# A transformer layer with pooling and RWKV-7 branches on one core: output product and second feed-forward product as seven block products instead of eight

## The reference, cut to what matters

```python
h = x * (1 + sc1) + sh1                       # x: 512 tokens x 1024, sc/sh/gt: from c @ w_ada
p = h @ w_in
y_pool = pool_branch(...)                     # ends in m @ w_pool_up, 512 x 1024
y_rwkv = rwkv7_branch(...)                    # ends in o @ w_rwkv_up, 1024 x 1024
g_pool, g_rwkv = split(sigmoid(p_gate))
mixed = (g_pool * y_pool + g_rwkv * y_rwkv) @ w_out         # 1024 x 1024
x = layer_norm(ALPHA * x + (1 + gt1) * mixed, ln1_g, ln1_b)
h = x * (1 + sc2) + sh2
f = square(relu(h @ w_ff1)) @ w_ff2           # 1024 x 4096, 4096 x 1024
x = layer_norm(ALPHA * x + (1 + gt2) * f, ln2_g, ln2_b)
```

## Time and profile before

| | us |
|---|---|
| median of 3 runs | 1107.34 |
| lowest, highest | 1106.0, 1109.77 |
| the profiled execution | 1106.47 |
| its span, first to last instruction | 1104.7 |
| matmul busy in the span | 999.9 |
| VectorE, ScalarE, Pool busy | 517.9, 413.8, 401.8 |
| mean granted TensorE clock | 0.957 |

### The profile page before, as it was taken

The page is one execution under the profiler, slowest core; times in us unless marked ns, Lnnn a source line. Parts: engine busy times, 40 slices in busy tenths (PEclk is TensorE's granted clock), DMA queues, the critical chain, the costliest instruction groups (busy, mean ns, idle before and its releaser), DMA issues.

```text
span 1104.7 us, 25425 instructions
## 1 busy us (share of the span) xinstructions
PE 999.9 (91%) x10997; PEld 798.8 (72%) x10997; DVE 517.9 (47%) x620; ACT 413.8 (37%) x500; POOL 401.8 (36%) x236
## 2 busy tenths in 40 slices
PE   1898998898899889997999999889999999999992
PEld 1676777685677678675688888768888888888881
DVE  6636589377748768743231245746112112112217
ACT  0335354356335532524433224375124224214311
POOL 6333412311311131125253443445434434443422
PEclk9799999999999899998899999879999999999996
DMA  9322333223323324321433543304333333333201
GB/s 370 106 77 63 97 117 102 79 79 94 93 79 98 103 60 118 105 76 39 133 100 101 160 114 107 95 1 132 97 94 97 96 96 91 99 95 93 79 1 76
DMA packets 153641, 108.08 MB, mean 98 GB/s; under 512 B 5395, under 2 KB 145601, under 8 KB 153537
## 3 DMA queue, kind: packets, MB, share of 16 engines
q1 hardware_dynamic: 143729, 83.46, 25.9%
q10 hardware_dynamic: 9808, 23.08, 6.9%
HBM read 100.23 MB, written 2.10 MB: 93 GB/s over the span
## 4 chain that ended last, share of the span: by engine, by line
PE 47%; DVE 4%; DMA 1%; ACT 1%; issue 0%; SPq 0%; POOL 0%; DVEq 0%; ACTq 0%; POOLq 0%
PE set L1757 23%; PE bank L1757 20%; PE bank L1859 1%; PE set L1859 1%; DVE G L1319 1%; DMA w_raw<-in_w_rwkv_up_dram 1%; DVE xt L1388 1%; DVE xt L1390 1%; PE set L1821 0%; DVE t L1304 0%; PE set L1838 0%; PE set L1607 0%; PE set L1606 0%; DVE aa L1322 0%; DVE stat L1348 0%
## 5 line engine op out<-in xcount | busy, mean ns | idle before, releaser
L560 POOL TENSOR_TENSOR w_lo<-w_raw,w_hi 128x1024 fp32r<-128x1024 f32 (+2 forms) x87 | 200.4, 2303 | 439.2 <-ACT w_hi L641 399.2
L616 POOL TENSOR_TENSOR w_lo<-w_raw,w_hi 128x1024 fp32r<-128x1024 f32 x48 | 115.8, 2413 | 145.9 <-ACT w_hi L936 145.7
L1460 PE MATMUL bank<-h_hi,w_hi 128*128 128x512 f32 x256 | 109.3, 427 | 2.1 <-POOL w_lo L560 2.0
L641 ACT ACTIVATE w_hi<-w_raw 128x1024 fp32r<-128x1024 f32 (+2 forms) x75 | 75.5, 1006 | 82.9 <-PE set L1757 43.6
L669 ACT ACTIVATE Q<-set 128x1024 f32<-128x1024 f32 x56 | 57.4, 1026 | 130.7 <-PE set L1514 73.8
L936 ACT ACTIVATE w_hi<-w_raw 128x1024 fp32r<-128x1024 f32 x60 | 63.7, 1061 | 110.7 <-PE bank L1757 53.9
L1460 PE MATMUL bank<-h_hi,w_lo 128*128 128x512 f32 x256 | 103.3, 403 | 0.3 <-issue 0.3
L1460 PE MATMUL bank<-h_lo,w_hi 128*128 128x512 f32 x256 | 103.5, 404 | 0.0
L1355 DVE TENSOR_TENSOR f<-t 128x512 f32<-128x512 f32 x32 | 26.4, 825 | 125.9 <-ACT t L945 125.5
L1757 PE MATMUL bank<-h_hi,w_hi 128*128 128x512 f32 x192 | 76.5, 398 | 0.0
L1757 PE MATMUL set<-y_hi,w_hi 128*128 128x512 f32 x192 | 76.1, 396 | 0.0
(11 more groups left out here) (328 smaller groups left out, 2030.3 us busy)
## 6 DMA issues: line engine op xcount, KB each, us to landing
w_raw<-in_w_ff_dram SPq DMA_DIRECT2D x64, 512.0 KB, 3.9
w_raw<-in_w_in_dram SPq DMA_DIRECT2D x46, 512.0 KB, 3.8
y<-in_w_ada_dram ACTq DMA_DIRECT2D x20, 512.0 KB, 4.0
ada<-in_w_ada_dram SPq DMA_DIRECT2D x16, 512.0 KB, 9.6
Q<-in_w_ada_dram ACTq DMA_DIRECT2D x12, 512.0 KB, 4.3
w_raw<-in_w_rwkv_up_dram SPq DMA_DIRECT2D x8, 512.0 KB, 4.3
w_raw<-in_w_out_dram SPq DMA_DIRECT2D x8, 512.0 KB, 3.8
xtok<-in_x_dram SPq DMA_DIRECT2D x4, 512.0 KB, 9.9
```

Source lines behind the costliest of these rows:

```text
L560: link(pool.tensor_tensor(part_of(k, w_lo), part_of(k, w_raw), part_of(k, w_hi).bitcast(F32), ALU.subtract), "lo_ready")
L616: again(pool.tensor_tensor(part_of(k, w_lo), part_of(k, w_raw), part_of(k, w_hi).bitcast(F32), ALU.subtract), "lo_ready")
L641: link(act.activation(part_of(k, w_hi), part_of(k, w_raw), ACT.Copy), "hi_ready")
L1460: mm = pe.matmul(o, w, hx, start=(m == 0), stop=(m == 3 * KT - 1))
```

## The change

**The seven products.** Left operand (tokens x features) and right operand (weights) are cut into 2 x 2 blocks, and the product is made by the scheme of Strassen and Winograd with seven block products instead of eight. One **unit** takes 512 of the inner features: left 512 tokens x 512, in halves of 256 tokens and 256 features; right 512 x 1024, in four quarters `B11`, `B12`, `B21`, `B22` of 256 x 512. The output product is two units, the second feed-forward product eight. A unit needs four sums of weights (`T1 = B12 - B11`, `T3 = B22 - B12`, `T2 = B22 - T1`, `T4 = B21 - T2`; VectorE, 128 x 1024 each), four sums of the left halves (`a_sum`, 128 x 256 for each of two groups of features), and seven products (`quarters`) of 2 x 2 x 3 = 12 matmuls, so 84 where the eight blocks took 96 for the same part. Now the activations are the stationary side and 512 columns of weights move.

**Layout.** The result is tokens x features. Products that share an output are accumulated in the same bank and read in between: `take` adds a bank to the tile `acc_out`, unscaled, 14 times a unit. The gate (`1 + gt1`, `1 + gt2`) is now a row over features: 16 transposes of a broadcast column in the last slots of the recurrence and two ScalarE copies make `gate1` and `gate2`. In the last unit of each product `last_takes` multiplies by the gate and adds to `res` (`merged`, `taken_last`), and takes the statistics with `bn_stats`, for both layer norms. `x_again` is no longer turned, and nothing is turned back; instead the normalised `x` is turned for `h2` (32 transposes). `ln1_g` and `ln1_b` are folded into the residual by VectorE (`residual`, 8 instructions) and Pool (8).

**Who makes what.** Of the eleven lo parts of a feed-forward unit (four chunks of `w_ff1`, m = 0 to 3, seven forms of `w_ff2`, m = 4 to 10) VectorE makes m = 2 to 6 (`low_tile`, while chunks are computed), Pool the others (mostly while the seven products run). In the output units Pool makes all. VectorE also makes the lo parts of the left side (`low_raw`, `low_sums`).

**Order.** TensorE does the first output unit after `pool_up(5)` and the second after `pool_up(7)`. A unit of the feed-forward stage is four chunks of `w_ff1` (24 matmuls each) and the seven products. The loop has six or seven turns by engine instead of two or three.

```diff
-        mix_hi, mix_lo = sb("mix_hi", [P, KT, S], F32R), sb("mix_lo", [P, KT, S], F32R)
+        a_hi, a_lo = sb("a_hi", [P, 7, 2, S // 2], F32R), sb("a_lo", [P, 7, 2, S // 2], F32R)
+        a_sum = sb("a_sum", [P, 4, S // 2])
...
+        FORMS = ("B11", "B21", "T2", "T1", "T3", "B22", "T4")
+        FORM_RAW = dict(B11=3, B21=5, T2=3, T1=8, T3=4, B22=6, T4=5)
...
+        PRODUCTS = ((0, 4), (2, 0), (5, 4), (4, 6), (1, 4), (6, 6), (3, 4))
+        OPENS = (True, True, False, True, False, False, False)
+        FREED_BY = (6, None, 0, 5, 2, 3, 4)
+        READ_INTO = ((0, 0), (0, 0), (0, 1), (2, 1), (2, 1), (0, 1), (2, 0))
+        A_READY = ((1, 3), (2, 4), (5, 7), (5, 7), (6, 8), (6, 8), (6, 8))
...
+        LO_BY_DVE = (2, 3, 4, 5, 6)
...
+            for k in (K_UP, K_UP + 1):
+                load_chunk(sp, k)
             sp.wait_ge(sem("y_ready"), QUADS)
...
+            with pool.Fori(0, NU - 1) as q:
+                for m in (0, 1, 7, 8, 9, 10):
+                    again(pool.tensor_tensor(w_lo[SLOT[m]][:, :, :], raw[:, :, :], w_hi[SLOT[m]][:, :, :].bitcast(F32), ALU.subtract), "lo_ready")
...
+            def a_sums(link, n):
+                i = n % 2
+                x0, x1 = left[:, i, 0:S // 2], left[:, i, S // 2:S]
+                if n % 4 < 2:
+                    link(dve.tensor_tensor(a_sum[:, 0, :], x0, x1, ALU.subtract), "a_summed")
+                else:
+                    link(dve.tensor_tensor(a_sum[:, 1, :], x1, right[:, S // 2:S], ALU.add))
+                    link(dve.tensor_tensor(a_sum[:, 2, :], a_sum[:, 1, :], x0, ALU.subtract))
+                    link(dve.tensor_tensor(a_sum[:, 3, :], right[:, 0:S // 2], a_sum[:, 2, :], ALU.subtract), "a_summed")
...
+            def take(link, unit, at, row, units=0):
+                wait_half(unit, at, row, units)
+                j, z = READ_INTO[at][0] + row, READ_INTO[at][1]
+                product = bank[PRODUCTS[at][1] + row]
+                if unit in (0, 2) and at in FIRST_READ:
+                    link(dve.tensor_copy(part(acc_out, j, z), product), "taken")
+                else:
+                    link(dve.tensor_tensor(part(acc_out, j, z), product, part(acc_out, j, z), ALU.add), "taken")
+            def merged(link, j, z, stage):
+                row = (gate1, gate2)[stage][:, z * S:(z + 1) * S]
+                link(dve.tensor_tensor(part(acc_out, j, z), part(acc_out, j, z), row, ALU.mult))
+                link(dve.tensor_tensor(part(res, j, z), part(res, j, z), part(acc_out, j, z), ALU.add))
...
+            def unit_sums(link, units):
+                for m in range(4):
+                    dve.wait_ge(sem("hidden_raw"), units * 4 + (4 + m + 1))
+                    a_sums(link, 12 + m)
+                    low_raw(link, 12 + m, units)
+                    if m < 3:
+                        low_tile(link, (2, 3, 5)[m], 1, units)
+                    low_sums(link, 12 + m, units)
+                    if m == 0:
+                        summed(link, "T1", 3, units)
+                        summed(link, "T3", 3, units)
+                    if m == 1:
+                        low_tile(link, 4, 1, units)
+                        summed(link, "T2", 3, units)
+                    if m == 2:
+                        summed(link, "T4", 3, units)
+                    if m == 3:
+                        low_tile(link, 6, 1, units)
...
+            def quarters(unit, k0, slots, free, units=0):
+                for at, (form, first) in enumerate(PRODUCTS):
+                    w = [two_by(half[slots[at]]) for half in (w_hi, w_lo)]
+                    for row in range(2):
+                        free(at, row)
+                        if at and FREED_BY[at] is not None and FREED_BY[at] < at:
+                            pe.wait_ge(sem("taken"), units * (2 * NFORM) + (2 * NFORM * unit + 2 * FREED_BY[at] + row + 1))
+                        for i in range(2):
+                            if row == 0:
+                                pe.wait_ge(sem("a_low"), units * 8 + (8 * unit + A_READY[form][i]))
+                            for m, (a, wx) in enumerate(((a_hi, w[0]), (a_lo, w[0]), (a_hi, w[1]))):
+                                mm = pe.matmul(bank[first + row], a[:, form, i, row * P:(row + 1) * P], wx[:, i, :],
+                                               start=OPENS[at] and i == 0 and m == 0, stop=i == 1 and m == 2, skip_group_check=True)
...
             for n in range(KT):
                 rwkv_up(n)
                 pool_up(n)
+                if n == KT - 3:
+                    out_unit(0)
+            out_unit(1)
...
+            quarters(2, K_UNIT[2], FIRST_SLOT[4:], ff_free(2, 0, 0))
+            with pe.Fori(0, NU - 1) as q:
+                for m in range(4):
+                    hidden_chunk(m, SLOT[m], q, 1)
+                quarters(3, K_UNIT[2] + PER, SLOT[4:], ff_free(3, q, 1), q)
```

851 lines of the change are left out of this document (531 added, 320 removed).

## The result

The changed kernel takes 1153.5 us (1153.3 to 1157.9), the kernel before 1106.8. Every median here is of the undisturbed executions; one of 4758.8 us of the changed kernel and one of 1422.4 us in e5 are left out. The ratio is 1.0425, with a 95% interval of 1.0398 to 1.0453. The forecast was 1126 us, 1090 to 1138: the direction was right, the size was not, and the time lies outside the range, 27.5 us above the forecast. The profiled execution took 1153.3 us with a span of 1151.6, against 1124.0 forecast and 1104.7 before.

A forecast was written before the change was run, and what follows sets the result against it. TensorE was taken to bound the kernel (91% busy), VectorE the two layer norms. 12.7 - 22.1 - 3.1 + 1.8 + 10 + 5 + 15 = +19.3 us on 1104.7 gave 1124.0 span, median about 1126; range 1090 to 1138 us.

The forecast's parts named there:

- the price of the first feed-forward unit (5): First feed-forward unit: waits for the second product, Pool's residual work and the take behind residual(0) cost 5 us, bounds 2 to 12.
- the choice of the gap in the loop (4): Loop units: TensorE waits 1.7 us in each of six, +10 us; 0.8 if gaps close, 3.5 with 0.17 us gaps.
- the sum of the bounds: Whole kernel: the bounds of the layer norm, loop, first unit and end were said to reach from 1090 to 1140 us.
- Start of the up-projection: Start of the up-projection: the first w_rwkv_up block is issued earlier, so rwkv_up(0) starts at 543.4 instead of 546.05 us.
- Matmuls, 0.230 us each: All ten units: 84 matmuls instead of 96 at 0.230 us; -5.5 us before the first layer norm, -22.1 us after.
- First layer norm, +12.7: Up to the first feed-forward product: VectorE's row, prolonged 18.4 us by eight Pool lo parts, ends at 736 us, +12.7 us.
- first rival: Two layer norms: Pool wins no gap in VectorE's row or its lo parts fall beside takes; 1096 us, chance 0.25.
- the likeliest case: Whole kernel: the forecast case, 1116 to 1137 us, chance 0.52.
- 35 us or more of idle TensorE: Sign of being right: a gap of 35 us or more, in pieces, between pool_up(7) and the first feed-forward product.
- slower still: Loop: each VectorE instruction carries 0.1 us more for register waits, +15 to +20 us, 1143 us; chance 0.10.
- The end, +15: Last unit to the end: takes, merging, statistics and Pool's lo parts leave 36.9 us after TensorE's share, not 21.7; +15 us.
- "slower": Whole kernel: the changed kernel is slower than before by more than 0.3%; chance 0.63.

The follow-up runs named there:

- e5: Changed kernel with VectorE instead of Pool making ten lo parts (seven of the second output unit, three of the first feed-forward chunks); 1147.0 us.
- e3: Changed kernel with Pool's ten lo parts (second output unit, first three feed-forward chunks) cut to 8 columns, work left out; 1134.9 us.
- e2: Changed kernel with VectorE's loop over six feed-forward units written out, so its waits are on constants; 1149.6 us.
- e4: Changed kernel with VectorE making T4 and low_tile(5) later in the loop units and the last unit; 1147.6 us.
- e6: e2 plus the residual work moved out of the first feed-forward unit, VectorE's behind its last take, Pool's into a later unit; 1145.3 us.
- e9: The changed kernel run again without an edit, to see what varies by itself; 1153.5 us, 1.038 of the kernel before.
- e8: Changed kernel with Pool's six lo parts per unit cut to 8 columns in the loop and last unit, work left out; 1145.4 us.
- e10: Changed kernel with merging and statistics of the last unit's first six products left out; 1136.4 us.
- e7: Changed kernel with the edits of e1, e2, e4 (in the first unit too), e5 and e6 together; 1130.1 us.
- e1: Changed kernel with low_tile(4) and ScalarE's split for it one step earlier in the first feed-forward unit; 1155.5 us.

## Why the prediction was right in direction and wrong in size

Two steps failed: the price of the first feed-forward unit (5) and the choice of the gap in the loop (4). A third one is the sum of the bounds, behind the terms. The terms by the numbers that the prediction gave them:

1. *Start of the up-projection, -2.6 us: right.* ScalarE no longer waits for the load of `w_rwkv_up`. From the recurrence's last transposes to `rwkv_up(0)` it is 25.3 us instead of 27.6 (518.44 to 546.05 in the earlier trace rows), -2.3. It didn't show in the trace's axis, since the recurrence ended 1.7 us later in this execution; across eleven executions of this front part that end lies anywhere between 514.6 and 528.3 us, so the 1.7 are no effect of the change that could be told from the spread.
2. *Matmuls, 0.230 us each: nearly.* 96 of the chunks take 22.19 us, 0.231 each. The last five block products take 13.97 us for 60, 0.233. The prediction left out that a block product could run slower; over a unit with its two restarts it comes to some 0.8 us (20.1 us for 84, waits taken off, against 19.3).
3. *First layer norm, +12.7: right in kind.* Without the 1.7 us of the recurrence the first feed-forward product is 1.9 us later than forecast. VectorE's row ends the stage, and Pool's lo parts prolong it by 17.1 us (e3). The first rival, in which Pool wins no gap or falls beside takes, is refuted by the ten meetings. The earlier trace rows were the right rows, and the likeliest case was rightly chosen by them. Small errors cancel in the sum: the parts add up to 717.2 and not 717.5, the last `x_hat` took 0.81 us (L1614) where it had 1.3, and there were ten meetings of 1.9 us on average, not eight of 2.3. It had named 35 us or more of idle TensorE between `pool_up(7)` and this product as a sign; 32.5 came.
4. *Loop unit, 1.7 us of waiting: mis-sized.* It is 2.5 us of waiting and about 0.8 of slower matmuls and restarts. The prediction had bounds of 0.8 us (every gap closes) and 3.5 us (every gap 0.17, as ScalarE's), and took a value near the first. The step that failed is that choice: the gaps of VectorE are 0.12 us at each wait for another engine. That is the mechanism of the rival "slower still", which I gave 0.10. Its direction is shown (e2: 0.83 us a unit), its size was 5 us in the loop and not 15 to 20. The second instruction of VectorE in the earlier trace rows also waits for ScalarE in a loop and has a gap of 0.04, and the prediction took this row for the rule. The same loop of the kernel before has the larger gap as well, at the other instruction, where ScalarE's result had been there for a while (at 750.72 and 756.36 us):

```profile
752.87 2.77 DVE L1357 TENSOR_TENSOR y_lo<-f,y_hi 128x512 fp32r<-128x512 f32 x1
755.77 0.69 DVE L1355 TENSOR_TENSOR f<-t 128x512 f32<-128x512 f32 x1
756.50 0.69 DVE L1357 TENSOR_TENSOR y_lo<-f,y_hi 128x512 fp32r<-128x512 f32 x1
757.31 0.69 DVE L1355 TENSOR_TENSOR f<-t 128x512 f32<-128x512 f32 x1
```

L1355 starts 0.12 to 0.13 us after L1357 ends, L1357 0.03 to 0.04 after L1355. So the trace that the prediction had in hand showed both gaps; why one of two waits in one loop is free of it stays open. The third product's wait of 1.0 us comes from the chain behind chunk 3 (e4) and had been counted as 0.5.

5. *First feed-forward unit, +5: the largest error, 12 us.* The waits are 12.5 us instead of 5, and the unit's 84 product matmuls take 24.7 us without them, where a loop unit's take 20.1: 4.5 us more, for which the prediction had no term. With the 12 us on top the loss is 17, beyond the range of 2 to 12 us. I had priced Pool's residual work at 1 us: it prolonged five VectorE instructions by 5 us ahead of the first product. I had let `residual(0)` cost 3.2 us, its own work, without its own two meetings with Pool's lo parts (2.1 us each). And I hadn't followed `low_tile(4)`, which stands behind chunk 2's sums in this unit alone. The prediction counted meetings one by one in the layer norm and not here, half a page later, by the same price. e6 shows what the residual work costs: 12.2 us of the unit against e9, of which 8.2 are waits and 3.9 slower matmuls; 2.2 come back in a later unit. The slower matmuls are the clock: see below.
6. *The end, +15: nearly right,* 80.9 instead of 78.3. Pool's three lo parts cost the 5.1 us that it had (e8); a fourth meeting, with Pool's row of output, adds 1.9. Merging and statistics on VectorE make the end long (e10).

The chances: "slower" was rightly the likeliest, but 0.10 for everything above 1138 us was too little. The range itself doesn't follow from its bounds. The upper ends of 3 to 6 (16.7, 21, 12 and 18 us) less 23.4 us of TensorE's work are +44 us, about 1152 us, and not the 1140 that the prediction wrote. Measured were 16.3 (3), 19.6 (4), 17 (5) and 17.8 (6): all near their upper ends, and one beyond. Nearly all the open costs lay on one engine, whose row gets longer by every one of them, so their upper ends belong together; I had treated them as independent.

No version of this change that I tried beats the kernel before. e7 is the best, at 1.018. In its loop a unit takes 43.28 us; the kernel before has 192 matmuls of 0.230 us in one, 44.2 us. So even repaired the change saves 0.9 of the 2.8 us that it takes off TensorE in each unit. The last unit to the end still takes 39.8 us more than the unit's matmuls (81.2 - 41.4), where 21.7 us followed the last product before.

## What to carry to other kernels

When work moves from an engine that is the bound to one that is half idle, write out the receiving engine's row stage by stage and don't go by its share: VectorE, 47% busy over the old kernel and 65% over the new, is 90% busy from 661 to 740 us, and there the 17 us that Pool's lo parts added to it were lost in full (e3). Price a meeting of VectorE (two inputs in SBUF) with Pool by rows like these (1.3 to 2.1 us for a Pool instruction of 2.4), count the meetings in every stage with the same care, and where there are many let VectorE do the work itself. If a chain on the receiving engine has no slack, moving one of its steps forward only moves the wait to the next consumer (e1).

## What the runs showed of the hardware that I had not expected

**A register wait costs 0.09 us.** In VectorE's loop an instruction that waits for another engine by a value from the loop's register starts 0.12 us after the one before it; with a constant it is 0.03 us (e2). By these numbers it takes some nine of them (an estimate) to make the 0.83 us a unit. One kind of wait in the old loop is free of it (4 above).

**The clock after a short wait differs from execution to execution.** TensorE waits 2.9 us for `O` and then does the last transposes and gate products of the recurrence. In all eleven traces of this code the granted clock falls to one half (1.2 instead of 2.4 GHz) at that wait or just behind it. In six of them it is back before the gate products, in five only in the middle of them, with the same code and the same wait. These are the stretches at half and at full clock up to `rwkv_up(0)`, of the changed kernel's first trace and of e2's:

```profile
519.30:532.90 13.60, 12.75 (x79) 6.04 (x80) 3.75 (x6) 2.82 (x5) 0.55 (x1) 0.50 0.21 63
532.90:546.00 13.10, 13.10 (x52) 9.50 (x51) 1.39 (x2) 6.81 (x9) 4.42 (x3) 1.00 0.81 257
```

```profile
519.30:522.80 3.50, 3.12 (x66) 2.29 (x66) 0.33 (x1) 0.98 (x2) 0.00 (x0) 0.51 0.77 225
522.80:541.00 18.20, 18.20 (x65) 11.68 (x64) 4.33 (x7) 8.69 (x13) 4.94 (x3) 1.00 0.59 187
```

It is worth 4.5 us (25.3 to 25.8 against 20.8 to 20.9 us). The Trainium skill, page TensorE: Matmul & The Clock Gate, section "What's actually happening", says that one kernel can show different numbers of slow matmuls from run to run, and speaks of the kernel's start. These traces agree, and show it in mid-kernel.

**The same in the first feed-forward unit.** With unchanged code it took 63.1, 67.1 (e9), 67.0 (e2), 64.0 (e4), 63.8 (e8), 67.2 us (e10) and, behind an edited stage, 67.0 (e3) and 60.7 (e5). Its 84 product matmuls, waits taken off, took 24.7 us in the first trace, 26.7 in e9, 22.8 in e6 and 22.5 in e7, and 20.1 in a loop unit. After most of its waits come matmuls at half clock (0.77 us for the first one of a row where 0.47 is the quick one), and how many varies. In e2 the last piece (24 matmuls) took 8.4 us at a granted clock of 0.63, in the changed kernel's trace 5.6 us at 1.00:

```profile
793.10:801.50 8.40, 8.40 (x24) 6.64 (x25) 6.83 (x10) 1.06 (x1) 1.78 (x1) 0.63 0.21 60
```

```profile
797.00:802.60 5.60, 5.59 (x24) 4.60 (x25) 5.39 (x7) 1.06 (x1) 2.84 (x2) 1.00 0.59 183
```

So a wait of some microseconds on TensorE costs more than its length. The prediction had no term for this in the first unit. Of the 12 us there some 4.5 are slow matmuls, an estimate from the rows (24.7 against 20.1 us); no run separates them from the waits that go ahead of them.

**Pool was never kept out.** The Trainium skill, page SBUF — State Buffer, section "Who interferes with whom", calls the shared ports an exclusive lock for the whole instruction, given to whoever issues first. The trace agrees that VectorE's instruction ends 0.56 us after Pool's (714.10 against 714.66), so that most of its 0.69 us lie behind Pool's end. What the prediction's first rival took from it, that a row of VectorE without holes could keep Pool out, is not so here: with VectorE's instructions 0.03 us apart, Pool had its turn after at most one of them.
